# Two entries of a hand-written order are rewritten: attention scores in pairs of heads, and the states turned back a slab later

## The reference

```python
for i in range(2):
    h = rmsnorm(x, norm_mix[i])
    q, k, v, cb, cc, cx, u, g = split(h @ w_in[i])
    q, k = partial_rope(q, cos, sin), partial_rope(k, cos, sin)    # 8 heads of q, 2 of k and v, 64 wide
    y_attn = sliding_window_attention(q, k, v, attn_sinks[i]) @ w_attn_o[i]
    y_conv = (cb * short_conv(cc * cx, conv_w[i])) @ w_conv_o[i]
    ys = gelu(s5_ssm(u, ...))                                      # a diagonal scan over time, complex
    y_ssm = (ys * sigmoid(ys @ w_ssm_glu[i])) @ w_ssm_o[i]
    gates = sigmoid(g + b_gate[i])
    x = x + (gates[0] * y_attn + gates[1] * y_conv + gates[2] * y_ssm) @ w_mix_o[i]
    x = x + swiglu(rmsnorm(x, norm_ffn[i]))
# sliding_window_attention: s = q k^T / 8 + mask, m = max(s, sink), p = exp(s - m),
# o = (p / (sum p + exp(sink - m))) v
```

## Time and profile before

| | us |
|---|---|
| median of 3 runs | 2145.69 |
| lowest and highest run | 2143.53, 2146.36 |
| the profiled execution, its own time | 2144.67 |
| span in the profile of that execution | 2142.9 |
| PE busy in the span | 2119.5 |
| DVE busy | 1639.8 |
| ACT busy | 1212.0 |

### The profile page before, as it was taken

The page is one execution under the profiler, slowest core; times in us unless marked ns, Lnnn a source line. Parts: engine busy times, 40 slices in busy tenths (PEclk is TensorE's granted clock), DMA queues, the critical chain, the costliest instruction groups (busy, mean ns, idle before and its releaser), DMA issues.

```text
span 2142.9 us, 47911 instructions
## 1 busy us (share of the span) xinstructions
PE 2119.5 (99%) x18724; PEld 2062.3 (96%) x18724; DVE 1639.8 (77%) x2626; ACT 1212.0 (57%) x1821; POOL 56.4 (3%) x54
## 2 busy tenths in 40 slices
PE   9999999999999999999999999999999999999998
PEld 8999999999999999899999999999899999999998
DVE  8997877987778766788947877776688947877764
ACT  6656544556656445456658845445446658845443
POOL 0000000000000000000002200000000002200000
PEclk9999999999999999999999999999999999999999
DMA  6434555644446556554544455556554544455553
GB/s 251 158 132 153 202 191 186 200 158 149 139 168 216 186 193 209 179 169 143 175 158 155 146 198 207 186 191 212 180 169 144 177 158 152 149 199 188 187 188 127
DMA packets 102976, 376.54 MB, mean 176 GB/s; under 512 B 11680, under 2 KB 11808, under 8 KB 102304
## 3 DMA queue, kind: packets, MB, share of 16 engines
q1 hardware_dynamic: 101664, 368.66, 50.6%
q10 hardware_dynamic: 1152, 5.58, 0.7%
HBM read 373.14 MB, written 1.05 MB: 175 GB/s over the span
## 4 chain that ended last, share of the span: by engine, by line
PE 91%; DVE 5%; ACT 2%; issue 1%; DMA 0%; DVEq 0%; ACTq 0%
PE acc L771 25%; PE acc L773 25%; PE acc L772 25%; DVE w_lo L1805 2%; PE acc L890 1%; PE acc L891 1%; PE acc L892 1%; PE acc L836 1%; PE acc L835 1%; PE acc L837 1%; PE mid L1227 1%; ACT w_hi L1325 1%; PE mid L1127 1%; PE mid L1213 0%; PE mid L958 0%
## 5 line engine op out<-in xcount | busy, mean ns | idle before, releaser
L1805 DVE TENSOR_TENSOR w_lo<-w_raw,w_hi 128x1024 fp32r<-128x1024 f32 x694 | 847.8, 1226 | 315.6 <-ACT w_hi L1325 307.3
L1325 ACT CAST w_hi<-w_raw 128x1024 fp32r<-128x1024 f32 x694 | 724.2, 1047 | 535.4 <-PE acc L773 477.2
L771 PE MATMUL acc<-h_hi,w_hi 128*128 128x256 f32 x2096 | 596.6, 285 | 0.3 <-DVE w_lo L1805 0.3
L773 PE MATMUL acc<-h_hi,w_lo 128*128 128x256 f32 x2096 | 585.5, 279 | 0.0
L772 PE MATMUL acc<-h_lo,w_hi 128*128 128x256 f32 x2096 | 584.3, 279 | 0.0
L771 PE MATMUL acc<-g_hi,w_hi 128*128 128x256 f32 x1456 | 409.3, 281 | 0.8 <-DVE w_lo L1805 0.7
L773 PE MATMUL acc<-g_hi,w_lo 128*128 128x256 f32 x1456 | 406.5, 279 | 0.0
L772 PE MATMUL acc<-g_lo,w_hi 128*128 128x256 f32 x1456 | 406.2, 279 | 0.0
L771 PEld LDWEIGHTS acc<-h_hi,w_hi 128*128 128x128 f32 x2096 | 394.1, 188 | 6.5 <-issue 4.7
L773 PEld LDWEIGHTS acc<-h_hi,w_lo 128*128 128x128 f32 x2096 | 393.9, 188 | 0.0
L772 PEld LDWEIGHTS acc<-h_lo,w_hi 128*128 128x128 f32 x2096 | 393.4, 188 | 0.5
(11 more groups left out here) (438 smaller groups left out, 3440.9 us busy)
## 6 DMA issues: line engine op xcount, KB each, us to landing
w_raw<-weights_d SPq DMA_DIRECT2D x695, 512.0 KB, 3.3
p<-p_d ACTq DMA_DIRECT2D x3, 1080.0 KB, 8.5
rdec<-decay_d ACTq DMA_DIRECT2D x2, 768.0 KB, 5.4
p<-p_d SPq DMA_DIRECT2D x1, 1024.0 KB, 10.6
out_d<-work SPq DMA_DIRECT2D x4, 256.0 KB, 2.3
x_all<-x_d SPq DMA_DIRECT2D x1, 516.0 KB, 4.4
w_raw<-weights_d SPq DMA_DIRECT2D x2, 256.0 KB, 5.8
x_all<-x_d SPq DMA_DIRECT2D x1, 512.0 KB, 6.1
```

Source lines behind the costliest of these rows:

```text
L771: mm(dst, wh, hi[:, k, :], start=first and j == 0, stop=False)
L773: done = mm(dst, wl, hi[:, k, :], start=False, stop=last and j == len(ks) - 1)
L1325: nc.scalar.copy(w_hi[:, slot, :], w_raw[:, slot, :]).then_inc(hi_done, 1)
L1805: tt(w_lo[:, slot, :], w_raw[:, slot, :], w_hi[:, slot, :].bitcast(F32), SUB).then_inc(lo_v, 1)
```

## The change

Only the two tables change. In each layer the eight heads' scores now follow in four pairs, each pair after one slab, where five places held them before (0; 1, 2; 3, 4; 5; 6, 7 in the first layer and 0, 1; 2; 3, 4; 5, 6; 7 in the second). The masks stand elsewhere too, and in the first layer `turn` stands behind slab 37 instead of 36. No instruction is added, removed or given another operand.

```diff
         30: (("rot", 2), ("rot", 3)),
-        31: (("scores", 0), ("mask", 0), ("scan",)),
-        33: (("scores", 1), ("scores", 2)),
-        34: (("mask", 1),),
-        35: (("mask", 2), ("scores", 3), ("mask", 3), ("scores", 4)),
-        36: (("mask", 4), ("turn",), ("scores", 5)),
-        38: (("scores", 6), ("scores", 7), ("mask", 5)),
+        31: (("scores", 0), ("scores", 1), ("mask", 0), ("scan",)),
+        34: (("mask", 1), ("scores", 2), ("scores", 3)),
+        35: (("mask", 2), ("mask", 3)),
+        36: (("scores", 4), ("scores", 5)),
+        37: (("mask", 4), ("turn",)),
+        38: (("mask", 5), ("scores", 6), ("scores", 7)),
...
         27: (("scores", 0), ("scores", 1)),
-        29: (("scores", 2), ("turn",)),
-        32: (("mask", 0), ("mask", 1), ("mask", 2)),
-        33: (("scores", 3), ("mask", 3), ("scores", 4)),
-        34: (("out_power", 1), ("mask", 4)),
-        36: (("out_power", 2), ("scores", 5), ("scores", 6), ("mask", 5)),
-        37: (("out_power", 3), ("mask", 6), ("scores", 7), ("mask", 7), ("maxima",)),
+        29: (("turn",),),
+        32: (("mask", 0), ("mask", 1), ("scores", 2), ("scores", 3)),
+        33: (("mask", 2), ("mask", 3)),
+        34: (("out_power", 1), ("scores", 4), ("scores", 5)),
+        35: (("mask", 4),),
+        36: (("out_power", 2), ("mask", 5), ("scores", 6), ("scores", 7)),
+        37: (("out_power", 3), ("mask", 6), ("mask", 7), ("maxima",)),
```

## The result

| | median | lowest to highest | runs | ratio to before |
|---|---|---|---|---|
| before | 2145.60 us | 2143.53 to 2147.71 | 8 | |
| after | 2152.93 us | 2147.95 to 2155.85 | 8 | 1.0031 [1.0022 to 1.0040] |

The changed kernel is slower by 7.3 us, 0.31%. The forecast was 2148.2 us, no measurable change, with a range from 2145.8 to 2151.0. The profiled execution took 2153.18 us, with a span of 2151.4; PE was busy for 2123.1 us of it, DVE for 1640.2, ACT for 1211.9. So PE, doing the same matmuls, was busy 3.6 us longer than in the earlier trace rows, and idle for longer too.

The account below looks back on a forecast made before the run. The prediction took PE as the bound, busy for 2119.5 of 2142.9 us. First layer 0.5 plus second layer 2.0 made 2.5 us, added to 2145.69 for 2148.2 us, with a range from 2145.8 to 2151.0.

Parts of the forecast that it names:

- A visit costs 1.05 us, one head or two: Both layers, PE between slabs: each visit to the scores costs 1.05 us; five visits become four, saving 1.05 us a layer.
- First layer, +0.5: First layer: the saving of 1.05 us is lost whole and `cx` starts at 162.94, so the layer is 0.5 us slower.
- the wait for the split of slab 45: First layer near 158 us: PE, 1.05 us ahead, stops for 1.3 us until DVE's split ends at 159.25.
- DVE's idle time ahead of the splits of slabs 39 and 40: First layer: DVE starts slab 40's split at 134.97 instead of 134.49, a new idle time of 0.48 us.
- Rival 2: PE's instruction supply: pauses without a releaser shrink or return in first layer's `cx`, up to 1.5 us either way; chance 0.12.
- Rival 4: First layer: the load of slab 40 comes late, so 0.5 becomes up to 1.5, giving 2149.2 us; chance 0.08.
- Second layer, +2.0: Second layer: PE idles 2.2 us at head 3's scores for head 0's mask; with 1.05 given back, 2.0 us slower.
- The cover on DVE: Second layer: DVE's last table comes near 562.5, ahead of `cx` at 565.8, so DVE's later start stays covered.
- DVE's own idle time behind mask 3: Second layer near 543 us: DVE waits for PE's slab 33 and ACT's rounding of slab 37, starting 2.3 us later.
- The failed step: Second layer, behind PE's 2.2 us idle time: the sum of 2.5 us went by rows with the clock granted in full (1.00).
- rival 3: The clock drops in the second layer's idle time, adding 2.8 us if for one slab, giving 2151.0; chance 0.10.
- Rival 1: Both layers: the waits don't bite and only the saving of 2.1 us is left, giving 2143.6 us; chance 0.06.

Follow-up runs that it names:

- mended first-layer tables: After with first layer's `scan` and last pair one slab later, `turn` behind slab 36, and second layer's second pair behind slab 33: ratios to before 0.9992 and 0.9993.

## Why the prediction was wrong, point by point

**A visit costs 1.05 us, one head or two: right.** In after, from slab to slab is 130.12 - 129.05 = 1.07 us with two heads, as forecast:

```profile
129.05 0.28 PE L774 MATMUL acc<-h_hi,w_lo 128*128 128x256 f32 x1
129.26 0.50 PE L1011 MATMUL mid<-qk 64*128 64x128 f32 x4
129.58 0.61 PE L1012 MATMUL mid<-qk 64*128 64x256 f32 x4
130.12 0.39 PE L772 MATMUL acc<-h_hi,w_hi 128*128 128x256 f32 x1
```

**First layer, +0.5: the mechanism right, the size too small.** The wait for the split of slab 45 was forecast at 1.3 us and measured at 1.19, and `cx` follows the third table (its last instruction ends at 164.71 + 0.68 = 165.39 on DVE, `cx` starts at 165.50). DVE's idle time ahead of the splits of slabs 39 and 40 grew from 1.02 us to 0.40 + 1.59, by 0.97 where 0.48 was forecast. But DVE also came about 0.56 us sooner against PE here (its `scan` starts 3.51 us behind the first score matmul, before 4.07), since PE had lost time at 106 us. So the split of slab 40 starts 17.76 us behind the first score, where the forecast's 134.97 is 17.74, and the third table comes 0.5 later than in the earlier trace rows. The term was read from one trace as 45.73 - 45.23; the runs show 0.4 to 1.05, since the old order has scatter that one trace hides. Behind `cx` the term was zero. The stretch there takes 1.3 us more in six of seven traces, most of it in pauses. Rival 2 named such pauses at up to 1.5 us, and gave them 0.12. Rival 4, a late load of slab 40, did not happen: ACT waited for PE, not for the load (136.06 and 136.44 in its rows above).

**Second layer, +2.0: right for the wait.** The wait is 2.16 us for 2.2, its growth by 1.15 with each split is shown, and with 1.01 us of waiting the sum holds to 0.01 us. The cover on DVE held too: the third table was done at 568.55 + 0.69 = 569.24 and `cx` came at 572.45, 3.2 us of slack for a forecast 3.3 (the forecast's "17.5 us to the last table" should read 17.0; its 562.5 goes by that):

```profile
568.55 0.69 DVE L2131 TENSOR_TENSOR ce_im<-tm 128x512 f32<-128x512 f32 x1
```

```profile
572.45 0.34 PE L979 MATMUL mid<-xst,cab 128*32 128x64 f32 x8
```

DVE's own idle time behind mask 3 was 3.85 us for a forecast 2.3. The 1.5 more is PE's slab 33 at half clock.

**The failed step: full clock behind the new idle time.** The sum took the 1.00 that the earlier trace rows show at 1.9 us of idle time and carried it on to what follows 2.2 us. That row covers only the idle time itself (102.80 to 104.70). In the same trace the clock does stay full behind it:

```profile
104.70:108.10 3.40, 3.38 (x47) 3.26 (x47) 3.00 (x4) 3.29 (x7) 0.00 (x0) 1.00 0.02 5
```

But that is one execution at one place. The prediction said that 2.2 us was beyond any row, named a clock under 1.00 behind 540 us as a sign of being wrong, and gave it 0.10 as rival 3. Its price is 1.55 us in the trace of after (3.55 less the 2.0 of the wait), 3.0 in the trace of the second layer's table alone, with the same wait (46.91 less 41.88 and 2.0), and over the 17 runs of after the mean clock is lower by 0.0013, which is 2.8 us, the price that rival 3 had (the half clock at the end of each execution makes this good to about 1 us, so the match is partly luck). The mechanism was found and priced; its chance was wrong, and so was leaving it out of the sum. And the row with 1.9 us on which the step leaned is itself on the edge, as the runs now show (below).

The Trainium skill (TensorE: Matmul & The Clock Gate, Part 1: The HAM clock gate) puts it that the point at which the clock changes shifts from run to run, as it depends on where the first matmul falls. The traces show a scatter of this kind, in how long half clock lasts: almost equal waits of 2.15 and 2.16 us gave 6.8 and 3.4 us of it. Whether for the reason that the Trainium skill gives, no run here tests.

**The sum again.** Over all runs after is 6.5 us above before (means of 17 and 85 runs). Some 2.8 is clock, 2.0 the second layer's wait, and 1.7 is left for the first layer. So of the 4.0 us by which this exceeds the forecast's 2.5 the failed step has some 2.8, the first layer 1.2. For the first layer the traces give 0.4 to 1.05 and 1.3 in six of seven. The two sets of runs of the first layer's table alone give 2.4 and 0.9. That last split is good to about 1 us and no better.

**The range was narrow** for a second reason. Single executions scatter, at places that the change doesn't touch, by as much as the range allowed (2.4 us below the forecast, 2.8 above). That alone doesn't put a median outside, since before has the same scatter; but the median of the second set of after, 2151.01, lies 1.9 us under the first and right at the range's end. In 8 of 14 traces PE ran at half clock for 3.4 us from about 106 us on, and the same eight have a pause of 0.4 to 0.9 us near 115.7; with the two the first scores come at 119.6 to 120.0 us, without them at 116.9 to 118.0. (Here too the load of instructions ahead of the pause is late: it begins at 113.3 to 113.7 us in the eight, at 109.9 to 110.9 in the other six.) The profiled execution of before was one without, that of after one with it:

```profile
105.15 0.54 PE L959 MATMUL mid<-u,bt 128*32 128x64 f32 x23 [2.18 <-issue]
```

```profile
105.50:108.90 3.40, 3.40 (x31) 3.31 (x20) 2.32 (x3) 3.32 (x6) 0.00 (x0) 0.55 0.02 5
```

The eight are kernels with old, new and mended first-layer tables (2 of 5, 5 of 7 and 1 of 2), so the change isn't needed for it. Whether it shifts the odds 14 traces can't show, but the mean clock of the first layer's table alone (0.9982, 0.9983) speaks against it. Comparing just the two profiles would have charged it with 2.5 us that nothing shows it to owe.

**Rival 1** (only the saving is left) did not come true in after. Where the mended tables take the waits away, its saving appears in part: 1.7 us of the 2.1.

## What to carry to other kernels

An idle time of the bottleneck costs its length and, in all five traces with 2.15 us or more at this place, a stretch at half clock behind it that cost 1.6 to 3.4 us more; price both as soon as a move makes a wait longer than any in the trace. Packing small matmuls side by side saves here 0.7 us of the 1.05 that a visit costs, and only where each visit still comes after what it waits for: here the pair behind the next slab did that. And where the time of one stretch hangs on loads, take it from several executions, since one trace can be at either end of its scatter.

## What the runs showed of the hardware

- **Idle time and clock.** At the second layer's scores: none behind 1.01 us of idle time in the one trace that has it; half clock behind 2.15, 2.16, 2.17, 3.31 and 3.43 us, all five. It lasted 3.4 us in two and 6.8 in three. At 104 us, behind 1.65 to 2.48 us without work, half clock in 8 of 14: there 1.91 us sufficed once and 2.44 did not twice. At 501 us half clock came behind 1.97 us, the longest idle time there, and behind none of the 13 of 1.41 to 1.85. In the second layer's `cx` idle times of up to 1.69 us had none behind them. So the length of the idle time alone doesn't decide.
- **What it costs.** At half clock a matmul of 128 x 256 in fp32r takes 0.213 us instead of 0.117, so 3.4 us at half clock are 16 matmuls instead of 29, or 1.5 us lost (1.55 in the trace of after).
- **The first layer's wait of 1.2 us** at slab 45 cost no clock: 0.9982 and 0.9983 on average for the two sets that have it and no other.
- **Pauses that no semaphore ends** (0.2 to 1.1 us, behind `cx`) appear in six of seven traces with one order of steps ahead of them and in none of seven with others. They go with a later load of instructions, and stayed unexplained.
